# A fused network of transformer and recurrent blocks on one core: column sums of the first norm ahead of the fourth weight slot, an unloaded padding, and modulation chunks moved from the first RWKV stage to the next FFN

## The reference, cut to what matters

```
mod = silu(c) @ ada_w[i] + ada_b[i]           # shift, scale, gate for three sub-layers of a block
h = rms_norm(x, g) * (1 + scale) + shift
ffn:  x += gate / 2 * ((silu(a) * b) @ w_out),  a, b = split(h @ w_in)       # d_ff 2816
rwkv: r, k, v, decay, a, g from token-shifted h; state = state*w + sa*(kk*a) + v*k; y = state @ r
```

## Time and profile before

| | |
|---|---|
| median of 3 runs | 3310.05 us (3298.89, 3310.05, 3310.62) |
| the profiled execution | 3311.3 us, of which the span in the trace is 3309.5 us |
| busy share of the span | PE 96%, DVE 70%, ACT 41%, POOL 3% |
| mean granted clock of PE | 0.955 of full speed |
| modulation chunks added by L471 | 154, mean 1812 ns |
| weight slots loaded by SP | 291, median 6.3 us from issue to landing |

### The profile page before, as it was taken

The page is one execution under the profiler, slowest core; times in us unless marked ns, Lnnn a source line. Parts: engine busy times, 40 slices in busy tenths (PEclk is TensorE's granted clock), DMA queues, the critical chain, the costliest instruction groups (busy, mean ns, idle before and its releaser), DMA issues.

```text
span 3309.5 us, 49163 instructions
## 1 busy us (share of the span) xinstructions
PE 3170.0 (96%) x19642; PEld 2734.8 (83%) x19642; DVE 2322.8 (70%) x3432; ACT 1353.8 (41%) x2160; POOL 96.9 (3%) x187
## 2 busy tenths in 40 slices
PE   7998988999999999999999999999989999999998
PEld 6886677888889888888887888886688888968888
DVE  5977855687886866878857888876652876642485
ACT  3533021454545753545444545533121544432353
POOL 0000000000000000000000000000000000000000
PEclk8998987999999999999998999999998999999899
DMA  8774421466675325675654666652201453433353
GB/s 332 256 274 162 175 96 68 179 233 248 241 283 214 140 96 219 239 280 215 255 223 148 235 258 238 235 187 96 107 1 43 187 191 131 158 151 120 148 191 127
DMA packets 69667, 610.48 MB, mean 184 GB/s; under 512 B 7728, under 2 KB 7888, under 8 KB 31696
## 3 DMA queue, kind: packets, MB, share of 16 engines
q1 hardware_dynamic: 42768, 460.46, 37.0%
q0 software_dynamic: 26352, 144.88, 11.6%
q10 hardware_dynamic: 336, 2.13, 0.2%
HBM read 605.34 MB, written 2.10 MB: 184 GB/s over the span
## 4 chain that ended last, share of the span: by engine, by line
PE 86%; DVE 9%; DMA 2%; issue 2%; ACT 1%; DVEq 0%; SPq 0%; POOLq 0%; ACTq 0%
PE psum L302 30%; PE psum L861 22%; PE psum L865 11%; PE psum L882 10%; PE psum L889 6%; PE psum L300 4%; PE psum L886 1%; DVE ada_sum L471 1%; DVE arena L749 1%; PE psum L1605 1%; DMA ada_in<-in_ada_w 1%; DMA weights<-in_weights 1%; PE psum L1554 1%; DVE arena L2185 1%; DVE wkv_base L1952 0%
## 5 line engine op out<-in xcount | busy, mean ns | idle before, releaser
L812 ACT ACTIVATE unit_high<-weights 128x1024 fp32r<-128x1024 f32 x594 | 630.1, 1063 | 752.4 <-PE psum L865 393.9
L818 DVE TENSOR_TENSOR unit_low<-weights,unit_high 128x1024 fp32r<-128x1024 f32 x594 | 725.4, 1223 | 219.2 <-ACT unit_high L812 218.8
L861 PE MATMUL psum<-h_part,unit_high 128*128 128x512 f32 x3168 | 820.7, 396 | 18.6 <-DVE h_part L736 12.0
L861 PEld LDWEIGHTS psum<-h_part,unit_high 128*128 128x128 f32 x3168 | 576.4, 191 | 127.3 <-issue 14.6
L865 PEld LDWEIGHTS psum<-h_part,unit_low 128*128 128x128 f32 x3168 | 445.3, 192 | 29.5
L865 PE MATMUL psum<-h_part,unit_low 128*128 128x256 f32 x3168 | 466.7, 284 | 0.0
L302 PE MATMUL psum<-arena,weights 128*128 128x256 f32 (+5 forms) x1936 | 421.3, 383 | 9.0 <-DVE arena L1851 5.1
L302 PEld LDWEIGHTS psum<-arena,weights 128*128 128x128 f32 (+4 forms) x1936 | 330.6, 193 | 93.2 <-issue 40.3
L882 PE MATMUL psum<-hidden,unit_high 128*128 128x512 f32 x1386 | 353.5, 396 | 0.0
L302 PEld LDWEIGHTS psum<-in_part,w_part 128*128 128x128 f32 x2400 | 303.7, 199 | 26.1 <-ACT arena L1120 13.0
L302 PE MATMUL psum<-in_part,w_part 128*128 128x256 f32 x2400 | 315.2, 292 | 7.0 <-issue 4.4
(11 more groups left out here) (289 smaller groups left out, 2643.1 us busy)
## 6 DMA issues: line engine op xcount, KB each, us to landing
weights<-in_weights SPq DMA_DIRECT2D x291, 1536.0 KB, 6.3
ada_in<-in_ada_w POOLq DMA_DIRECT2D x182, 768.0 KB, 5.8
consts<-in_consts POOLq DMA_DIRECT2D x1, 1696.0 KB, 14.4
x<-in_x SPq DMA_DIRECT2D x1, 1024.0 KB, 15.2
v_first<-arena ACTq DMA_DIRECT2D x1, 1024.0 KB, 3.9
arena<-v_first ACTq DMA_DIRECT2D x1, 1024.0 KB, 4.9
out<-x SPq DMA_DIRECT2D x1, 512.0 KB, 2.7
out<-x SPq DMA_DIRECT2D x2, 256.0 KB, 2.3
```

What stands on the lines that cost most here:

```text
L812: k.nc.scalar.activation(k.unit_part[0][:, n % UNIT_RING], w, ACT.Copy).then_inc(k.sem["unit_high"], 1)
L818: k.nc.vector.tensor_tensor(k.unit_part[1][:, n % UNIT_RING], w, k.unit_part[0][:, n % UNIT_RING].bitcast(FP32), ALU.subtract).then_inc(k. ...
L861: mm(k.psum[:, 2 * (j % 2) + half, :].rearrange("p (i t) -> p i t", i=2), lhsT=part(2 * j + half, 0, t), rhs=k.h_parts[:, :, t], start=t = ...
```

## The change

**Opening.** `first_mod_products` sums the squares before group 2, step 2, that is before the first block of slot 3, instead of before group 3. `stream_weights` writes the loads of slots 3 to 5 out and loads of slot 5 only the 8 blocks that hold weights (512 KB in place of 1536).

**First RWKV stage.** Unit 3 leaves its last five chunks (`LATE_CHUNKS`) to the FFN behind. Five calls of `beside` ahead of the values are gone: two between the decay and the key norms, and one of two behind each of the first three `base`. One call is added behind `values(1)`. Sums, copy, turn and columns of unit 2 move from the gate products to the beginning of the second unit of heads, and use PSUM banks 6 and 7.

**FFN behind it.** `early_mod(2)` no longer holds. The five late chunks of unit 3 are added at j = 1, 3, 5, 7, 9, the sums on PE stand before the products of j = 11, the turn at j = 13. Unit 4 has 4 chunks in the up half (`ADA_UP_LATE`) and 12 in the down half, where it had 7 and 9.

```
 def stream_weights(k, sp, w, slots):
-    with sp.Fori(1, slots // RING) as g:
+    for r in range(RING):
+        n = BLOCKS * P if r < RING - 1 else OPENING_BLOCKS % BLOCKS * P
+        sp.wait_ge(k.sem["weights_used"], r + 1)
+        sp.dma_start(k.weights[:, r, 0:n], w[RING + r, :, 0:n]).then_inc(k.weights_loaded[r], 16)
+    with sp.Fori(2, slots // RING) as g:
...
     for r in range(4):
-        if r == 3:
-            pe.wait_ge(k.sem["inputs_loaded"], 32)
-            norm_sums(k, pe, pr, 0)
         for t in range(KT):
+            if (r, t) == (2, 2):
+                pe.wait_ge(k.sem["inputs_loaded"], 32)
+                norm_sums(k, pe, pr, 0)
...
 def early_mod(n):
-    return 2 <= n < NORMS - 1
+    return LATE_MOD <= n < NORMS - 1
...
     for j in range(1, FT):
+        if n + 1 == LATE_MOD and j == LATE_SUMS_AT:
+            mod_sums(k, pe, pr, LATE_MOD, range(6))
+        if n + 1 == LATE_MOD and j == LATE_SUMS_AT + 2:
+            turn_mod_rows(k, pe, pr, LATE_MOD)
...
+        elif late and j in LATE_UP:
+            ada_sum(k, dve, LATE_MOD, ADA_STEPS - LATE_CHUNKS + LATE_UP.index(j))
...
-    units = [(u, i) for u in (2, 3) for i in range(ADA_STEPS)] if j == 0 else []
+    units = [(u, i) for u in (2, 3) for i in range(ADA_STEPS - LATE_CHUNKS * (u == 3))] if j == 0 else []
...
     v.tensor_tensor(z.sg, z.cum, z.sg, sub).then_inc(s["rw_cum"], 1)
-    beside()
     for t in range(4, KT):
         ins = scaled_key(t)
-        if t == 5:
-            beside()
...
     base(0, beside)
-    beside(2)
+    beside()
     base(1, gate_mixes)
-    beside(2)
+    beside()
     base(2, bonus)
-    beside(2)
+    beside()
     base(3, scaled_both)
```

More of the change, by code:

```diff
@@ L36 @@
 ADA_OPEN = 6
+OPENING_BLOCKS = 2 * KT * KT
 FIRST_UNIT = 1
@@ L39 @@
 UNITS_UP = 2 * FT
+LATE_MOD = 3
+LATE_CHUNKS = 5
 FFN_UNITS = 3 * FT
@@ L544, in mod_bank @@
 def mod_bank(u):
-    return 0 if u == 1 else 2 if u >= 3 else 3
+    return 0 if u == 1 else 6 if u in (2, LATE_MOD) else 2 if u > LATE_MOD else 3
 def turn_bank(u):
-    return 0 if u == 1 else 7 if u >= 3 else 3
+    return 0 if u == 1 else 7 if u >= 2 else 3
 def mod_products(k, pe, pr, u):
@@ L878, in down @@
                     pe.wait_ge(sem["x_ready"], KT * n + d - 3)
-            if f == 0 and d == 3 and unit is not None:
-                pe.wait_ge(sem["mod_ready"], unit + 1)
+            if f == 0 and 2 <= d < 4 and (unit is not None or n + 1 == LATE_MOD):
+                pe.wait_ge(sem["mod_ready"], n + 2)
             if d < KT - 1:
@@ L969 @@
 GATE_UP_FIRST = (2, 4, 6, 8, 10, 12)
+LATE_UP = (1, 3, 5, 7, 9)
+LATE_SUMS_AT = 11
+ADA_UP_LATE = (14, 16, 18, 20)
+ADA_DOWN_LATE = (0, 1, 3, 4, 6, 7, 9, 11, 12, 14, 15, 17)
 def ffn_vector(k, dve, own, i, n, unit=NORMS, gate=None, parts=None):
     base, first, v, sub = FT * i, FFN_UNITS * i, k.nc.vector, ALU.subtract
-    up, down = (ADA_UP_FIRST, ADA_DOWN_FIRST) if unit == FIRST_UNIT else (ADA_UP, ADA_DOWN)
+    late = n + 1 == LATE_MOD
+    up, down = ((ADA_UP_FIRST, ADA_DOWN_FIRST) if unit == FIRST_UNIT else (ADA_UP_LATE, ADA_DOWN_LATE) if late else
+                (ADA_UP, ADA_DOWN))
     def half_sum(j, half, to):
@@ L1000, in ffn_vector @@
             gate_sum(k, dve, GATE_UP_FIRST.index(j))
+        elif late and j in LATE_UP:
+            ada_sum(k, dve, LATE_MOD, ADA_STEPS - LATE_CHUNKS + LATE_UP.index(j))
+        elif late and j == LATE_SUMS_AT + 1:
+            mod_rows(k, dve, LATE_MOD)
+        elif late and j == LATE_SUMS_AT + 2:
+            mod_columns(k, dve, own, LATE_MOD)
         elif j in up:
@@ L1428, in rw_products @@
            done("g1", 1) if t == KT - 1 else None)
-    if j == 0:
-        pe.wait_ge(s["wk_near_read"], 2 * UNITS)
-        mod_sums(k, pe, pr, 2, range(6))
     for m in range(KT):
@@ L1441, in rw_products @@
             mm(k.psum[:, bank_of("v2", m), 0:T], w[32:64, P:2 * P], z.lora[32:64, 4], True, True, done("v2", m))
-    if j == 0:
-        turn_mod_rows(k, pe, pr, 2)
     def bonus_sums():
@@ L1616, in rw_products @@
     turn_values(0)
-    if j == 0:
-        pe.wait_ge(s["mod_ready"], 3)
     x32(head)
@@ L1627, in rw_products @@
     pe.wait_ge(s["rw_turned_read"], 2 * (j + 1))
+    if j == 0:
+        mod_sums(k, pe, pr, 2, range(6))
     for n in range(1, UNITS):
@@ L1637, in rw_products @@
         upper(tail)
+        if n == 1 and j == 0:
+            turn_mod_rows(k, pe, pr, 2)
         level16(head)
         across(tail)
+        if n == 1 and j == 0:
+            pe.wait_ge(s["mod_ready"], 3)
         x32(head)
@@ L2091, in rw_vector @@
     open_y(head)
[L2092 to L2095, removed]
+    beside(2)
     values(0)
@@ L2109, in rw_vector @@
     keys(head, 1)
-    beside()
+    if j == 0:
+        mod_rows(k, dve, 2)
     for n in range(1, UNITS):
         head, tail = chunks[n], chunks[n - 1]
+        if n == 1 and j == 0:
+            mod_columns(k, dve, own, 2)
         level16(head)
```

## The result

The changed kernel takes 3291.06 us (median of 19 runs, 3283.36 to 3309.84), the kernel before 3307.13 us (19 runs, 3298.89 to 3310.91). The ratio, estimated from all these runs, is 0.9962, 95% interval 0.9949 to 0.9974, which is 12.6 us less (8.6 to 16.9); the plain difference of the medians is 16.1, that of the means 12.8. The forecast was 3297 us, range 3286 to 3304, and 13.9 us less. Of the 6 us between 3297 and the median, 2.9 come from the starting point: the three runs of before that I had gave 3310.05, the nineteen give 3307.13. The runs of the changed kernel spread over 26 us, those of before over 12.

What follows compares the result with a forecast made beforehand. PE's products, 86% of the chain, bound the kernel, so only PE's waits could shrink. Terms -5.0 -3.7 -5.2 -2.5 +0.2 +1.5 +0.8 = -13.9 us gave 3297.4 from 3311.3, 3296.2 from the median; forecast 3297, range 3286 to 3304.

Steps and rivals of the forecast that it cites:

- Opening, -5.0: Start of the kernel: earlier sums of squares let ACT round the first FFN weights at 35.0 instead of 40.04 us.
- bounds of 3.2 and 5.9: Opening's gain: 3.2 us with all sums at half clock, 5.9 with the upper clock throughout, limited by slot 4's landing.
- Padding, 0 against before and 1.4 the price of a full load: Opening, slot 5: short load gains 0 against before but lets the sums move; a full one lands 1.4 us late.
- Key norms, -3.7: First RWKV stage: two chunks gone from DVE ahead of the key norms shorten PE's 7.1 us wait by 3.7.
- base, -5.2: First RWKV stage: chunks gone ahead of units two to four cut PE's 7.7 us of waits for `base` by 5.2.
- Levels, +0.2: First RWKV stage: new chunk behind the values +0.7, a chunk now first -0.8, the turn +0.3; together +0.2 us.
- Sums in the FFN and idle norm, +1.5 and +0.8: FFN of sub-layer 2: unit 3's sums between products that never wait, +1.5 us; longer half clock after the idle norm, +0.8.
- Clock, -2.5: First RWKV stage: shorter waits give back clock, 0 to 5.0 us behind key norms and `base`; middle taken, -2.5.
- the first (-18.1, the clock comes back everywhere): Opening keeps the upper clock and shorter RWKV waits no longer lower it: -18.1 us, 3292; chance 0.26.
- the second (-7.5, only waits): Sums at half clock, slot 5 late by 1.4, every low stretch stays: -7.5 us, 3302; chance 0.20 together with the fourth.
- The third rival, the FFN at the lower clock: PE cools in sub-layer 2's norm, the following FFN stays at the lower clock; eleven units give some 3327 us; chance 0.03.
- the fourth, nothing gained in the opening: Slot 6 held up by slot 4's landing or h, removing the opening's 5.0 us: 3301; chance 0.20 together with the second.

Runs made afterwards that it cites:

- experiment 3: Changed kernel with slot 5 loaded in full (1536 KB instead of 512); 3295.32 us, ratio 0.9965 to the kernel before.
- key chunks back: Changed kernel with the two chunks ahead of the key norms put back, the stage's last two calls doing nothing; 3289.71 us, ratio 0.9949 to the kernel before.
- all in stage: Changed kernel with stage chunks moved to DVE's waits, LATE_CHUNKS = 0, FFN behind as before; 3279.01 us, ratio 0.9915 to the kernel before.
- experiments 5 and 6: Changed kernel with, first, two chunks back ahead of the key norms, 3289.71 us; second, a chunk more behind each of the first three base, 3296.33 us.
- experiment 1: Kernel before with only the opening's part of the change; 3304.16 us, ratio 0.9992 to the kernel before.
- experiment 8: Changed kernel with six products that nobody reads in PE's wait for the key norms; 3290.49 us, ratio 0.9959 to the kernel before.
- experiment 11: Changed kernel with stage chunks moved to DVE's waits, all of unit 3's chunks kept in the stage, FFN behind as before; 3279.01 us, ratio 0.9915 to the kernel before.

## Why the prediction was right, step by step

*Opening, -5.0:* right in its mechanism, too large by 1.3. It is -3.7 in the profiled executions, inside the bounds of 3.2 and 5.9; over all traces the first FFN product lies at 38.0 to 40.8 us with the new opening and the short slot 5 (ten, mean 39.8) and at 41.1 to 44.2 with the old opening (three, mean 42.9), so in the mean the gain is 3.1. The step that was off is the sums: they begin 0.4 later and take 6.15 for 5.1, because I let the clock fall at 21.9 us as before and it fell at 21.4. The two traces in which it falls at 22.4 and 22.9 (key chunks back, all in stage) have the earliest first FFN products, 38.0 and 38.6. The upper bound is a slip: by its own rows, slot 4 there at 26.9 against 33.04, it is 6.1 and not 5.9.

*Padding, 0 against before and 1.4 the price of a full load:* the first held, the second was too low. In experiment 3 the full load was asked for at 28.07, not 26.0, since the sums began later and were longer, and took 7.1 us, not 6.2; PE waited 3.17 us. The first FFN product then came 3.7 us later.

*Key norms, -3.7, and base, -5.2:* the waits fell by 3.8 and 5.3 us, and came back with the chunks (experiments 5 and 6). In full-speed parts they are 2.8 and 4.5, where part of the waits lay at the lower clock already.

*Levels, +0.2:* not separately shown; PE's waits from 396 to 600 us went from 18.7 us to 19.9. The whole stage gives -7.0 in its full-speed part, against -7.3 by the two terms as measured.

*Sums in the FFN and idle norm, +1.5 and +0.8:* the FFN from norm to norm is 1.5 us longer. From the first FFN product to the next sums it is 2.0 longer (143.5 for 141.5), and the sums (1.52) and the turn (0.40), which the term left out, are all of that. Ahead of it the norm got 0.45 shorter, with no more of the lower clock counted than before (5.1 us in both), so the +0.8 was not there. No late chunk costs PE anything, as the sum had it.

*Clock, -2.5:* the term that carries the luck. Without it the measured terms are -3.7 -7.0 +1.5 = -9.2, and the ratio gives -12.6, so the clock gave 3.4, with the interval's width of 4 us either way, which does not exclude nothing. Near the waits it did give something back, from 11.9 us to 6.8 or 8.5, so 3.4 to 5.1. But it was not quite where I placed it. I expected the two stretches behind `base` to give up to 4.3 us and the one behind the key norms at most 0.7. Behind `base` the second went in every trace (1.7 us) and the first stayed at 3.4 us in three of four; behind the key norms 3.4 us came back in three of four, and nothing in the fourth. Behind 394 us a stretch came that cost 10 us, or half of that, or did not come, and I had no term for it. That the sum came within 1.3 us of the measured difference is thus in part luck: the opening gave 1.3 less than its term, the stage's waits 1.6 less by the split, and what the clock gave and took is not resolved.

*Rivals.* By the ratio both the first (-18.1, the clock comes back everywhere) and the second (-7.5, only waits) lie just outside the interval of -8.6 to -16.9. Single executions lie at either: the fastest of the changed kernel is 24 us below the median of before, the slowest 3 above. The third rival, the FFN at the lower clock, did not happen, and the fourth, nothing gained in the opening, is excluded by the traces of the changed kernel and of experiment 1.

The Trainium skill, TensorE: Matmul & The Clock Gate, Part 1, makes activity what releases the lower clock. The traces stay against the simple reading here: in the changed kernel the sums kept PE busy from 22 to 26 us at 0.50, in the kernel before PE was busy all of 521 to 540 us at 0.50, and six products in a wait did not hold the upper level (experiment 8).

## What to carry to other kernels

Here side work on an engine cost about its duration where another engine waited for that engine (experiments 5 and 6), and next to nothing in the traces where it waited itself (experiment 11: 1.1 us for five chunks more); so read both engines' waits before placing it, and count how fast its loads come, for a chunk that waits for its load moves the wait to the other side. A short load can be what makes a reordering pay, as slot 5 did in the trace. And where the clock differs between executions, one pair of traces proves no difference of a few us, even if the totals match the sum: split off what the lower clock took, check the split on stages that did not change, or take a second trace of each.

## What the runs showed of the hardware that was not expected

The granted clock and the products' durations disagree at the start of a program. In experiment 8's opening the clock column stands at 1.00, but 48 products take the 2.79 us that they take at 0.50 in the earlier trace rows, and the sums 6.96, as at 0.50 before:

```profile
11.00:14.00 3.00, 2.19 (x44) 1.00 1.02 434
...
22.00:24.00 2.00, 2.00 (x11) 1.00 1.00 424
```

```profile
11.89 2.79 PE L305 MATMUL psum<-weights,ada_sum 128*32 128x128 f32 x48 [0.81 <-DMA weights<-in_weights]
...
20.61 6.96 PE L303 MATMUL psum<-consts,arena 128*128 128x4 f32 x32 [2.23 <-ACT arena L635]
```

In the changed kernel's trace the second and third slots took 1.52 us each. So up to the first fall that the column shows, the durations are the evidence.

Unchanged stages moved by several us between traces: the one from the sums at 955 to those at 1290 us took 330.3 to 334.7 us, that from 2161 to 2561, with the second RWKV stage in it, 390.6 to 400.0, of which the lower clock took 23.9 to 34.1. In the middle of a stage PE was at 0.50 for some 20 us without a break although it never stood idle (kernel before, 520 to 541 us), so not every low stretch has a wait in it.
